# Starting the expert stage of a two-layer block after two heads' choice instead of eight

## The reference, cut to what matters

```python
def peer_ffn(hid, wq, sub_k1, sub_k2, expert_u, expert_v):
    ...
    def block(xb):                                     # xb: 128 tokens
        q = (xb @ wq).reshape(tb, PEER_HEADS, 2, half)           # 8 heads, two halves of 128
        s1 = jnp.einsum("thd,nd->thn", q[:, :, 0], sub_k1)       # 128 keys for each half
        s2 = jnp.einsum("thd,nd->thn", q[:, :, 1], sub_k2)
        v1, i1 = lax.top_k(s1, PEER_TOPK)                        # 16 of 128
        v2, i2 = lax.top_k(s2, PEER_TOPK)
        cand_s = (v1[..., :, None] + v2[..., None, :]).reshape(tb, PEER_HEADS, 256)
        cand_i = (i1[..., :, None] * PEER_NKEYS + i2[..., None, :]).reshape(tb, PEER_HEADS, 256)
        top_s, pos = lax.top_k(cand_s, PEER_TOPK)                # 16 of 256 pairs
        eid = jnp.take_along_axis(cand_i, pos, axis=-1).reshape(tb, 128)
        gate = jax.nn.softmax(top_s, axis=-1).reshape(tb, 128)
        a = jnp.einsum("td,tkd->tk", xb, expert_u[eid])          # 128 gathered rows a token
        w = (jax.nn.gelu(a, approximate=False) * gate).astype(xb.dtype)
        return jnp.einsum("tk,tkd->td", w, expert_v[eid])
```

## Time and profile before

| | |
|---|---|
| median of 3 runs | 5128.58 us (5128.55 to 5143.53) |
| profiled execution | 5135.76 us, its span 5133.9 us |
| PE busy | 3469.6 us (68%) |
| DVE busy | 3215.2 us (63%) |
| GpSimd busy | 1479.5 us (29%) |
| gathers | 1280, with 1347.13 MB on their queue |

### The profile page before, as it was taken

One profiled execution on the slowest core, in us unless ns is written; L12 is line 12 of the kernel. 1 busy time (PEld: TensorE's weight loads), 2 busy tenths in 40 slices (PEclk: granted clock), 3 DMA queues, 4 the chain that ended last, 5 costly groups with the idle time before them and its releaser, 6 DMA issues.

```text
span 5133.9 us, 49877 instructions
## 1 busy us (share of the span) xinstructions
PE 3469.6 (68%) x16644; PEld 1503.5 (29%) x16644; DVE 3215.2 (63%) x8195; ACT 656.7 (13%) x2167; POOL 1479.5 (29%) x1376
## 2 busy tenths in 40 slices
PE   6899999844688555455455558999857754555555
PEld 1476644511123111111111115855532211111111
DVE  1162322688778887887876661513378888788666
ACT  2131110200101101001000011211100110100101
POOL 0000000034434444344434430000024444443443
PEclk7877698867799877778777768778779877777776
DMA  7100032589999999999999961011269999999998
GB/s 275 43 1 25 13 115 86 212 325 415 416 414 406 413 401 420 413 412 416 409 410 421 421 282 43 1 33 37 86 253 417 411 417 411 412 411 410 419 421 347
DMA packets 293057, 1500.97 MB, mean 292 GB/s; under 512 B 25304, under 2 KB 86360, under 8 KB 128960
## 3 DMA queue, kind: packets, MB, share of 16 engines
q0 software_dynamic: 185888, 1347.13, 63.7%
q1 hardware_dynamic: 88912, 129.53, 7.4%
q10 hardware_dynamic: 18000, 21.12, 1.2%
HBM read 1489.20 MB, written 8.49 MB: 292 GB/s over the span
## 4 chain that ended last, share of the span: by engine, by line
PE 36%; DMA 30%; DVE 18%; issue 11%; ACT 2%; POOL 2%; DVEq 0%; POOLq 0%; ACTq 0%; SPq 0%
DMA X<-in_uv_dram,X 28%; PE ps L462 8%; PE ps L833 8%; PE ps L612 4%; PE ps L649 3%; DVE X L1521 3%; PE ps L624 2%; POOL X L1630 2%; DVE hT L1529 2%; DVE X L1437 1%; DVE X L1439 1%; DVE X L1440 1%; DMA wring<-in_ada_w_dram 1%; PE ps L677 1%; PE ps L687 1%
## 5 line engine op out<-in xcount | busy, mean ns | idle before, releaser
L833 PE MATMUL ps<-X,hT 64*64 64x512 f32 x2560 | 1678.0, 795 | 1433.7 <-DVE hT L1529 1433.4
L1630 POOL DMA_INDIRECT X<-in_uv_dram,X x1280 | 1404.1, 1097 | 2299.4 <-PE ps L836 1711.8
L1521 DVE CUSTOM_DVE_ANT_0 X<-yT,X 128x1024 f32<-128x1024 f32 x1280 | 1543.1, 1224 | 594.6 <-DMA X<-in_uv_dram,X 561.9
L836 PE MATMUL ps<-X,hT 64*64 64x512 f32 x2560 | 1678.6, 795 | 0.0
L835 PE MATMUL ps<-X,hT 64*64 64x512 f32 x2560 | 1678.5, 795 | 0.0
L834 PE MATMUL ps<-X,hT 64*64 64x512 f32 x2560 | 1678.3, 795 | 0.0
L833 PEld LDWEIGHTS ps<-X,hT 64*64 64x64 f32 x2560 | 373.0, 166 | 2671.9 <-DVE hT L1529 2045.3
L1146 ACT ACTIVATE X<-X 128x1 f32<-128x1 f32 x1280 | 258.8, 203 | 2963.5 <-DVE X L1521 2843.4
L1529 DVE TENSOR_SCALAR hT<-wukv,X 128x64 f32<-128x64 f32 x1280 | 434.7, 340 | 29.7 <-ACT X L1146 2.2
L836 PEld LDWEIGHTS ps<-X,hT 64*64 64x64 f32 x2560 | 373.4, 166 | 0.0
L835 PEld LDWEIGHTS ps<-X,hT 64*64 64x64 f32 x2560 | 373.2, 166 | 0.0
(11 more groups left out here) (237 smaller groups left out, 3227.1 us busy)
## 6 DMA issues: line engine op xcount, KB each, us to landing
wring<-in_ada_w_dram SPq DMA_DIRECT2D x48, 1024.0 KB
wring<-in_peer_wq_dram SPq DMA_DIRECT2D x32, 1024.0 KB
wring<-in_w_in_dram SPq DMA_DIRECT2D x24, 1024.0 KB
X<-in_uv_dram,X POOLq DMA_INDIRECT x1280
wring<-in_w_out_dram SPq DMA_DIRECT2D x8, 1024.0 KB
X<-mods ACTq DMA_DIRECT2D x14, 512.0 KB, 8.5
X<-scores SPq DMA_DIRECT2D x48, 128.0 KB, 7.0
yT<-mods ACTq DMA_DIRECT2D x8, 512.0 KB, 10.4
```

Source lines behind the costliest of these rows:

```text
L833: pe.matmul(ps[0:HD, h, :], dg(slice(0, HD), s), v0[0:HD], **ends)
L836: m = pe.matmul(ps[0:HD, 2 + h, :], dg(slice(HD, P), s + 1), v1[HD:P], **ends)
L1521: v.tensor_tensor_reduce(uvr[:, slot, 0:D], h2[:, t, :], uvr[:, slot, 0:D], 1.0, 0.0, ALU.mult, ALU.add, adot[:, s_:s_ + 1]).then_inc(S("d ...
L1630: g.indirect_dma_start(uvr[:, slot, :], None, a["uv"], bass.IndirectOffsetOnAxis(ap=istages[i % 2][:, s:s + 1], axis=0)).then_inc(S(f"uv{s ...
```

## The change

1. **Two heads before the first dot.** Queries, key scores and choice of heads 0 and 1 come ahead of tile 0 of a layer (`HEADS_UPFRONT = 2`). Heads 2 to 7 are made inside tile 0: three query blocks a pair (`BLOCKS_A_PAIR`), the key scores two pairs after a half's last block, `scores_in` five pairs after it, the indices at pairs 12, 17, 22, 28, 33 and 38 (`chosen_at`). PE's, ACT's and DVE's programs all get these steps after the pair's own work.
2. **Gates head by head** in tile 0: each head has a subtraction, an Exp on ACT over 16 elements, a sum, a reciprocal and a product.
3. **Tile 1's choice** is still made inside tile 0, at 24 listed pairs from 18 to 59 (`SECOND_STEPS`), with working tiles of its own (`kept_2`).
4. **One query group in layer two**: `FIRST_GROUP = (CT, TILES - CT)`, so all four tiles' queries (512 columns) are made at once, `peer_wq` is sent once, and the scores of three tiles go through DRAM.
5. **Pair diagonals**: DVE waits for both gelus of a pair, multiplies the two with their gates in one small instruction (semaphore `wt`), and makes both diagonals in one `tensor_tensor` over 2 times 64 elements. The ring of diagonals has 8 places and lies in `X`.
6. Semaphores follow (`istg0`, `istg1` by the tile's parity), the gate tables of the residual share one place, and the score loads wait for each head's stores.

```diff
-FIRST_GROUP = (CT, 1)
+FIRST_GROUP = (CT, TILES - CT)
+HEADS_UPFRONT = 2
+BLOCKS_A_PAIR = 3
+SECOND_STEPS = (18, 19, 23, 24, 25, 29, 30, 34, 35, 39, 40, 42, 43, 45, 46, 48, 49, 51, 52, 54, 55, 57, 58, 59)
+SECOND_GATES_AT = 60
-DGRING = 16
+DGRING = 8
...
+def query_done(n_, j):
+    if n_:
+        return next(q for q in range(REST_PAIRS) if KD * 2 * PH * (q + 1) // REST_PAIRS >= KD * (j + 1))
+    return (KD * (j + 1) - 1 - 2 * KD * HEADS_UPFRONT) // BLOCKS_A_PAIR
+def keys_at(n_, j):
+    return query_done(n_, j) + 2
+def scores_at(n_, j):
+    return query_done(n_, j) + 5
+def chosen_at(h):
+    return scores_at(0, 2 * h + 1) + 2
...
@@ in the program of SP @@
-                    for q in range(2 if len(group) > 1 else 0):
-                        sp.wait_ge(S(f"sd{q}"), B(f"sd{q}", L) + 16 * PH * stored)
                     for t in group[1:]:
+                        i = t - lo
                         for h in range(PH):
-                            sp.wait_ge(S("istg"), B("istg", L) + PH * (t - lo) + max(h - 1, 0))
+                            for q in range(2):
+                                sp.wait_ge(S(f"sd{q}"), B(f"sd{q}", L) + 16 * (PH * stored + h + 1))
+                            if h >= 2:
+                                sp.wait_ge(S(f"istg{i % 2}"), B(f"istg{i % 2}", L) + PH * (i // 2) + h - 1)
...
-                load_scores(first, 1)
-                for c in range(4):
-                    send(L, a["peer_wq"][L], c * CH, "fq", 2 * PH + 4 * (c + 1), False)
+                load_scores(first, 0)
+                if rest:
+                    for c in range(4):
+                        send(L, a["peer_wq"][L], c * CH, "fq", 2 * PH + 4 * (c + 1), False)
...
@@ in the program of PE @@
-                for j in range(2 * PH):
+                for j in range(2 * HEADS_UPFRONT):
                     for k in range(KD):
                         query(first, 0, j, k)
...
-                        if i == len(first) - 1:
+                        if i == 0:
+                            for j in range(2 * HEADS_UPFRONT, 2 * PH):
+                                if keys_at(0, j) == q:
+                                    key_scores(first, 0, j)
+                            b0 = 2 * KD * HEADS_UPFRONT + BLOCKS_A_PAIR * q
+                            for b in range(b0, min(blocks, b0 + BLOCKS_A_PAIR)):
+                                query(first, 0, b // KD, b % KD)
+                        if rest and i == len(first) - 1:
...
@@ in the program of ACT @@
+                def exp_head(h):
+                    act.wait_ge(S("gx"), B("gx", L) + h + 1)
+                    nc.scalar.activation(gx[:, 1, h * TOPK:(h + 1) * TOPK], gx[:, 0, h * TOPK:(h + 1) * TOPK], ACT.Exp).then_inc(S("ge"), 1)
...
+                        for j in range(2 * HEADS_UPFRONT, 2 * PH if i == 0 else 0):
+                            if keys_at(0, j) == q:
+                                query_out(first, 0, j)
+                            if scores_at(0, j) + 1 == q:
+                                store_scores(first, 0, j)
+                            if j % 2 and chosen_at(j // 2) == q:
+                                exp_head(j // 2)
...
@@ in the program of DVE @@
+                for h in range(HEADS_UPFRONT):
+                    for j in (2 * h, 2 * h + 1):
+                        scores_in(first, 0, j)
+                    v.wait_ge(S("fse"), B("fse", L) + 2 * h + 2)
+                    choose_keys(staged, (0, 1))
+                    indices(0, h)
+                    head_gates_out(h)
+                    head_gates_in(h)
...
-                        for s_ in range(q * BATCH, (q + 1) * BATCH):
-                            v.wait_ge(S("gel"), B("gel", L) + SLOTS * i + s_ + 1)
-                            if s_ >= DGRING:
-                                v.wait_ge(S("em"), B("em", L) + NQ * i + (s_ - DGRING) // 2 + 1)
-                            v.tensor_scalar(dg(slice(0, P), s_), ident2, agel[:, s_:s_ + 1], gstage[:, s_:s_ + 1], ALU.mult, ALU.mult).then_inc(S("dg"), 1)
+                        s_ = q * BATCH
+                        both = slice(s_, s_ + BATCH)
+                        v.wait_ge(S("gel"), B("gel", L) + SLOTS * i + s_ + BATCH)
+                        v.tensor_tensor(adot[:, both], agel[:, both], gstage[:, both], ALU.mult).then_inc(S("wt"), 1)
+                        if s_ >= DGRING:
+                            v.wait_ge(S("em"), B("em", L) + NQ * i + (s_ - DGRING) // 2 + 1)
+                        v.wait_ge(S("wt"), B("wt", L) + NQ * i + q + 1)
+                        v.tensor_tensor(dgs[:, s_ % DGRING:s_ % DGRING + BATCH, :], ident2.unsqueeze(1).to_broadcast([P, BATCH, HD]),
+                                        adot[:, both].unsqueeze(2).to_broadcast([P, BATCH, HD]), ALU.mult).then_inc(S("dg"), 1)
...
+                        if i == 0:
+                            for h in range(HEADS_UPFRONT, PH):
+                                for j in (2 * h, 2 * h + 1):
+                                    if scores_at(0, j) == q:
+                                        scores_in(first, 0, j)
+                                        v.wait_ge(S("fse"), B("fse", L) + j + 1)
+                                    if scores_at(0, j) + j % 2 == q:
+                                        choose_keys(staged, (j % 2,))
+                                if chosen_at(h) == q:
+                                    indices(0, h)
+                                    head_gates_out(h)
+                                if chosen_at(h) + 1 == q:
+                                    head_gates_in(h)
+                            if q in SECOND_STEPS:
+                                step = SECOND_STEPS.index(q)
+                                choose_loaded(step // 3, step % 3, kept_2)
```

More of the change, by code:

```diff
@@ L1134, in _, with load_gate @@
                         act.wait_ge(S(f"ms{q}"), B(f"ms{q}", L + 1) + 16 * (ADA_CHUNKS // 2))
[L1135 to L1139, removed]
+                def load_gate(s):
+                    act.dma_start(gtab, mods[L, s:s + 1, 5 * D:6 * D].partition_broadcast(P).rearrange("a b (c d) -> a (b c) d", d=NCTX)).then_inc(S("gt2"), 16)
+                if L < LAST:
+                    load_gate(0)
+                else:
+                    load_gate(1)
+                    act.dma_start(final_gain, a["final_norm_g"].partition_broadcast(P).rearrange("a b (c d) -> a (b c) d", d=NCTX)).then_inc(S("gt2"), 16)
                 def expert_gelus(i, ahead):
-                    with_rest = i == len(first) - 1
+                    with_rest = rest and i == len(first) - 1
+                    gates_at = SECOND_GATES_AT if i == 0 else REST_GATES_AT if with_rest else GATES_AT
                     for q in range(SLOTS // BATCH):
@@ L1478, in _ @@
                 link(v.tensor_tensor(ident2, ident[:, 0:HD], ident[:, HD:P], ALU.add))
-                for j in range(2 * PH):
-                    scores_in(first, 0, j)
-                    if j % 2:
-                        v.wait_ge(S("fse"), B("fse", L) + j + 1)
-                        choose_keys(staged, (0, 1))
-                        indices(0, j // 2)
-                gates_ahead(0)
+                for h in range(HEADS_UPFRONT):
+                    for j in (2 * h, 2 * h + 1):
[5 more added lines that the diff above has]
+                    head_gates_in(h)
                 NQ = SLOTS // BATCH
@@ L1530, in tile_body, with choose_loaded @@
                         if i and q == 1:
                             accumulate(i - 1)
-                        step = (q - CHOOSE_FROM) // CHOOSE_EVERY
-                        h, part = step // 3, step % 3
-                        if ahead and not with_rest and (q - CHOOSE_FROM) % CHOOSE_EVERY == 0 and 0 <= h < PH:
+                        def choose_loaded(h, part, kept=(v12, i12)):
+                            if part == 0:
+                                loaded = i if i + 1 < len(first) else i - 1
+                                v.wait_ge(S(f"sl{h % 2}"), B(f"sl{h % 2}", L) + 16 * (PH // 2 * loaded + h // 2 + 1))
@@ new lines, in tile_body @@
+                        if i == 0:
[14 more added lines that the diff above has]
+                                choose_loaded(step // 3, step % 3, kept_2)
+                        elif with_rest:
+                            for j in range(2 * PH):
+                                if scores_at(1, j) == q:
+                                    scores_in(rest, 1, j)
+                                    v.wait_ge(S("fse"), B("fse", L) + 2 * PH + j + 1)
+                                if scores_at(1, j) + j % 2 == q:
+                                    choose_keys(staged, (j % 2,))
+                                if j % 2 and scores_at(1, j) + 2 == q:
+                                    indices(i + 1, j // 2)
+                        elif ahead and (q - CHOOSE_FROM) % CHOOSE_EVERY == 0 and 0 <= (q - CHOOSE_FROM) // CHOOSE_EVERY < 3 * PH:
```

(3 more changed lines are left out.)

124 lines of the change are left out of this document (63 added, 61 removed).

## The result

The changed kernel takes 5161.8 us in the median of five runs (5160.8 to 5162.9), the kernel before 5133.1, now the median of five (5128.6 to 5143.5) and 4.5 more than the median of three given above. The ratio is 1.0053, with a 95% interval of 1.0038 to 1.0068: about 27 us slower, clear of what this kernel's measurement can tell from none. The profiled execution has a span of 5159.7 us, against 5133.9.

What follows compares the result with a forecast made beforehand. It took the gathers' DMA engines to bound the kernel before, and DVE tile 0 after the change. Terms 4 - 6 + 21 - 6 = +13, less 2, gave +11: 5147 us profiled, 5140 against the median; range 5113 to 5168.

Steps and rivals of the forecast that it cites:

- within 0.3%: Whole kernel: time hardly changed, within 15 us of before; chance 0.48.
- the forecast's own range: Whole kernel: 5122 us with a pair at 2.88 us, to 5158 us with a pair at 3.26.
- rival (a): Later tiles: a pair at 3.2 us or more makes DVE bind their choosing part, 5168 us; chance 0.18.
- First dots: Ahead of tile 0: first dot at 981.8 in layer one, 67 us earlier; 3754.5 in layer two, 45 earlier.
- The pair: DVE, pair that waits for no landing: 3.09 us instead of 2.88, 0.21 more; bounds 2.88 and 3.26.
- DVE's sum for tile 0: DVE's work in tile 0: 378 us in layer one, 382 in layer two, plus waits of 16 and 4.
- The late score load: Tile 0, pair 18: DVE waits 4 us for tile 1's scores, queued behind the last peer_wq half; bounds 0 and 10.
- Given back: End of tile 0: ring full when DVE's excess ends at pair 59; minus 6 us in each layer.
- Sum: Both layers: 4 - 6 + 21 - 6 = +13, less 2 for faster halves: +11 us.
- (b): Tile 0 of layer two: PE binds if its granted clock is 0.8; +10 us, 5150; chance 0.10.
- (c): Tile 0: gelu wait overlaps, a pair costs 2.6 us, 28 us saved in each layer, 5084; chance 0.07.
- (d): Tile 0 stays bound by gathers, so the earlier first dots are kept: -67 - 45 + 2, 5019 us; chance 0.03.

Runs made afterwards that it cites:

- the first experiment: Changed kernel with tile 1's score loads for heads 0 and 1 issued ahead of the last peer_wq chunk: 5140.4 us, ratio 1.0006 to the kernel before.
- late heads: Changed kernel with one narrow diagonal a slot and tile 1's heads 5 to 7 chosen inside tile 1: 5075.6 us, timed again 5069.0 us.

## Why the prediction was right where it was, and where not

The range held the time, and the mechanism was the one forecast: what is saved ahead of the stages is spent in tile 0, because DVE becomes its bound. But the likeliest case, "within 0.3%", did not come; slower, to which 0.42 was given, did. The range held in part by luck: 5161.8 is past 5158, the end of the forecast's own range, and inside 5168 only by what rival (a) had added, which fell. Counted from the kernel before, the 27 us are just inside the 29 of its own range. One of the signs that it had named came true, a wait of DVE for scores of more than 10 us. Step by step:

- **First dots.** From the first gather 12.7 us in layer one, as forecast. From PE's start 50.2 us in layer two (3707.1 to 3757.3) against 52. Forecast -67 and -45, measured -67 and -47.
- **The pair.** 3.12 to 3.17 us against 3.09. The wait for the gelu and the small product were as worked out; the next dot starts up to 0.06 later. About 3 us a layer.
- **DVE's sum for tile 0.** Forecast with all waits 398 and 402 us, measured 403.7 and 410.2. The light pairs' waits of 16 came out at 16.6 and 18.5. They reach to pair 11, where the forecast had ended them at pair 9.
- **The late score load** is the term that was mis-sized. I took 4 us with bounds of 0 and 10; it was 11.8 and 14.2, past the bound in both layers. From the timelines and the line of the load, in layer one of the kernel after: pair 15's diagonals, PE's key scores and the query blocks that follow them, SP's issues, and the load's time to landing.

```profile
1063.06 0.29 DVE L1598 TENSOR_TENSOR X<-wukv,X 128x128 f32<-128x128 f32 x1
...
1066.80 0.71 PE L828 MATMUL ps<-keysT,X 128*128 128x128 f32 x4
1067.35 1.46 PE L817 MATMUL ps<-hT,wring 128*128 128x256 f32 x6
...
1068.84 0.37 SPq L389 DMA_DIRECT2D wring<-in_peer_wq_dram  x1
1069.33 3.23 SPq L438 DMA_DIRECT2D X<-scores  x2
...
DMA to landing us min/median/max: 28.4/28.4/28.4
```

  DVE's way from pair 15 to its request was 22.8 us (1069.3 + 28.4 - 11.8 - 1063.1), forecast as 24. The load's way was forecast as 28 with its issue; 28.4 is what it took from the issue, and the issue itself came 6.3 us after pair 15's diagonals in layer one and 9.0 in layer two (3843.1 to 3852.1), as PE has that pair's products, key scores and queries to do before it releases SP. This way from DVE over PE to SP is what the forecast had left out: it let the load start with pair 15. The load's move in the first experiment took off 24 us, more than the 16 between forecast and measurement.
- **Given back.** Minus 6 in each layer was forecast. Tile 1 is 3.7 us shorter than before in layer one (344.6 against 348.3) and 6.3 in layer two (323.9 against 330.1). About right.
- **Sum.** Layer one -67.1 + 76.6 - 3.7 = +6, layer two -47.1 + 74.6 - 6.2 = +21, together 27. The forecast had +11. Of the 16 between, 14 are tile 0's, of which the score load is 26 - 8 = 18 and the rest minus 4.
- **A reading.** The two tiles whose ends the prediction reads for 328.6 us are tiles 1 and 2 of layer two, not of layer one as it says. Tiles 2 and 3 of layer one took 328.4 each, so nothing hangs on it.
- **Rivals.** (a) fell: tiles 2 to 5 of layer one took within 2 us what they took before, and the pair form alone costs the kernel before nothing. (b) fell: in tile 0 of layer two no wait of DVE for PE is among those of 0.2 us and more, and with the choice left out PE kept up at 345 us. (c) fell: no pair came near 2.6. (d) fell, for the reason given; when DVE's work was left out or carried on, the DMA engines were full again in tile 0, but with 5049 and 5069 us, not with its 5019.
- **Two rules.** By the Trainium skill, "VectorE: DVE Perf Modes" (Mode 2x_2P and What auto-detection actually checks), the streaming of a pair would cost 0.07 us more, an estimate from that page. The pair's 0.24 to 0.29 comes mainly from the wait and the second instruction, as the rows show, and the rule's share can't be told in them. By the Trainium skill, "ScalarE: Activation LUTs" (What ACT_TABLE_LOAD costs), a table switch costs 2.66 us. The traces do not show this: Exp started 1.30 us after its load did, and DVE had no wait for a head's gates above 0.3 us. ACT in layer two, before tile 1's gates:

```profile
4155.44 1.28 ACT L1200 ACT_TABLE_LOAD   x1
4156.74 0.31 ACT L1200 ACTIVATE X<-X 128x128 f32<-128x128 f32 x1
```

## What to carry to other kernels

Before an idle stretch is filled by moving work, add up the work of the in-order engine that must do it, up to the point where the bound of the steady state takes over again; filling the hole is worth only what that engine's sum leaves, however early the first product comes. Where a formerly slack engine becomes the bound, each of its small waits and each transfer queued behind a big one is to be priced anew, also those that an edit does not touch: here one load behind 1 MB cost 24 us, and an instruction form that was free before cost 21 to 27. The way out was to carry the excess to stretches with slack, not to make the first stretch start later.

## What was not expected of the hardware

A full DMA share and a bound DVE can stand side by side. With late heads the DMA engines were used to 1.00 and 0.99 behind pair 27 of the two tiles 0, and yet DVE waited for no landing there, and the 0.24 to 0.29 us a pair cost as much as with DVE alone as the bound, 23 to 27 us against 21 to 27. The ring of nine slots did not average this out. Why the two limits lie so close together there was not tried.
